# Hybrid decoder layer on one core: k's low part written once for two attentions, one projection copy moved to ScalarE, the down projection in token form

## The chip, the cores and the metric

The kernel runs on one core of a Trainium2 chip. The time is the device time of one execution in microseconds (us), as the median of several runs. The execution that the profiler recorded is one further run; its rows give times from the first instruction, and its span ends with the last one.

The names of the engines: PE is TensorE (PEld its weight loads), DVE is VectorE, ACT is ScalarE, POOL is GpSimd, SP is SyncE, which issues all the DMAs of this kernel.

## The reference

One decoder layer on 512 tokens of width 1024, in float32:

```python
a = rms_norm(h, attn_norm_g)
(nq, nkv, ngate, dq, dk, dv, fq, fk, fv, ff, mg) = split(a @ w_in)
# A: native sparse attention (compressed blocks, selected blocks, sliding window), 8 heads, gates from ngate
# B: differential attention, 4 heads x 2 maps;  C: forgetting attention, 8 heads, decay from ff
qb = rms_norm(dq per head of 64) * scale;  kb = rms_norm(dk per head of 64)
qc = rms_norm(fq per head of 64) * scale;  kc = rms_norm(fk per head of 64)
merged = gates[0] * (o_a @ w_br[0]) + gates[1] * (o_b @ w_br[1]) + gates[2] * (o_c @ w_br[2])
h = h + merged @ w_o
u, g = split(rms_norm(h, ffn_norm_g) @ w_up)         # 2816 features each
h = h + (gelu(causal_conv3(u)) * g) @ w_down
```

With 512 tokens the eight selected blocks are all the blocks there are, so the selected attention is causal attention over everything.

## The kernel before

**Precision.** A float32 product is made of three matmuls on fp32r operands. Each operand is cut into a high part (ACT rounds it, suffix `_h`, `wh`) and a low part (DVE subtracts the high part from the original, suffix `_l`, `wl`). The function `passes(dst, a_h, a_l, b_h, b_l, ...)` (L1278) issues high by high (L1280), high by low (L1281) and low by high (L1282). The first operand is the stationary one, the second moves through the array.

**Weights.** They come as 72 blocks of 128 x 2048 floats (1 MB each) through a ring of three raw buffers. ACT's `split` (L581, instruction at L588) writes `wh`, DVE's `split` (L849, instruction at L855) writes `wl` over the raw slot. SP loads a block when the block three places before has been used.

**The order of the work** is written out by hand for each engine, one instruction stream each, tied by semaphores. `place` gives each result its PSUM bank and its turn in it; `free` waits until a bank's result has been read, `full` until it has been written. The stages are: norm and transposes of x; for each of the three mixers (NSA, DIFF, FOX) its projections, its attention (a table of events in which gate-projection matmuls fill between the small attention steps) and its branch projection; the output projection; the FFN's up projection in 11 steps; the down projection in 11 blocks; the output.

**The start of NSA.** PE projects `cmp` (banks 6 and 7), `small` (32 columns for the gate and forget logits, bank 3), then the first half of `nq` for four token tiles into banks 0, 1, 2 and 3. The result of `small` is copied to `smT` by DVE (L917). In DVE's stream the copy stands behind `post(m, "cmp")` and the split of block `nq1`. PE then transposes `smT` (L1318), runs the first layer of the compression (`w1_sb` by `cpe`, L1335) and projects the second half of `nq`.

**q and k in DIFF and FOX.** After its norm a projection is transposed in four chunks of 128 columns (two heads of 64 each), each chunk by four PE transposes into bank 4 or 5 in turn (L1308). For k, ACT writes the high part of each head twice, into both halves of the partitions of `k_hh` (L656). DVE's `post_t` (L943 to L962) then writes the low part twice too:

```python
n = 2 * (chunk - 4) + e
hi = k_hh[home, n, :]
lows = [k_ll[home, n, :], k_ll[other, n, :]]
```

`q_hl` holds q's high part in a head's home half and its low part in the other half. So a score is one matmul with `k_hh` (high and low q by high k, L1422) and one with `k_ll` (high and low q by low k, L1423). Both `k_hh` and `k_ll` have eight heads' slots of 128 x 512. For NSA only slots 0 to 3 are used, and there both halves of `k_ll` are filled by one instruction (L864). DVE's stream after a k chunk pair is: 8 writes, the split of block `gate0`, 8 writes. On PE the first score of the attention waits until all chunks have been read (L1460 to L1464).

**The down projection** (`down`, L1603) has the stationary operand from the weights and the tokens moving, so the result for output columns `d` (8 groups of 128) has the features on the partitions and 512 tokens along the row, one bank each:

```python
cols = slice(d * P, (d + 1) * P)
ins = passes(ps[d][:, :], h[:, k, cols], l[:, k, cols], acts[k][0], acts[k][1], ...)
```

In the last block each finished bank is copied to `yT` (even `d` by ACT, L836, odd `d` by DVE, L1224), transposed back by four PE transposes (`finish`, L1597, two groups later in PE's stream), added to the residual `hid` into `outt` by DVE (L1217), and stored by SP in four stores of 256 columns each (L567).

Of the kernel before, what the change touches and what calls it, by code (L numbers as in the profile page):

```python
# [20 lines left out]
P = 128  # L21
S = 512
# [166 lines left out]
def build(nc, x, wblk, w1, w2, params, consts, out):  # L189
# [88 lines left out]
    for d in range(KD):  # L278
        plan(("YT", d), d)

    with ExitStack() as ctx:
# [73 lines left out]
        yT = at("yT", [P, KD, S], f32, 0)  # L355
        outt = at("outt", [P, TT, D], f32, 32 * KB)
# [77 lines left out]
        const_ready = sem("const_ready")  # L434
        cpe_ready = sem("cpe_ready")
# [101 lines left out]
        def _(sp):  # L537
# [27 lines left out]
            for n in range(4):  # L565
                sp.wait_ge(out_ready, 2 * n + 2)
                sp.dma_start(outv[:, :, n * 256:(n + 1) * 256], outt[:, :, n * 256:(n + 1) * 256]).then_inc(out_done, 16)  # L567
            sp.wait_ge(out_done, 64)
# [3 lines left out]
        def _(act):  # L572
# [125 lines left out]
            for m in (NSA, DIFF, FOX):  # L698
# [3 lines left out]
                if m == NSA:  # L702
                    split(BI[(m, "nq0")])
                    split(BI[(m, "nq1")])
# [128 lines left out]
            for d in range(0, KD, 2):  # L833
                full(act, ("Y", d))
                b = place[("Y", d)][0]
                nc.scalar.activation(yT[:, d, :], ps[b][:, :], ACT.Copy).then_inc(psum_free[b], 1)  # L836


        @block.vector
        def _(dve):  # L840
# [25 lines left out]
            def post(m, name):  # L866
# [47 lines left out]
                elif name == "small":  # L914
                    full(dve, ("P", m, name, 0))
                    b = place[("P", m, name, 0)][0]
                    nc.vector.tensor_copy(smT[:, :], ps[b][0:32, :]).then_inc(psum_free[b], 1)  # L917

            def post_t(m, name, part=0):
# [23 lines left out]
                for c in T_CHUNKS.get(name, [])[2 * part:2 * part + 2]:  # L943
# [7 lines left out]
                    for e in range(2):  # L951
# [4 lines left out]
                        else:  # L956
                            n = 2 * (chunk - 4) + e
                            hi = k_hh[home, n, :]
                            lows = [k_ll[home, n, :], k_ll[other, n, :]]
# [50 lines left out]
            for m in (NSA, DIFF, FOX):  # L1010
                units = units_of(m)
                if m == NSA:
# [3 lines left out]
                    post(m, "small")  # L1016
# [197 lines left out]
            def finish(d):  # L1214
                full(dve, ("YT", d))
                cols = slice(d * P, (d + 1) * P)
                nc.vector.tensor_tensor(outt[:, :, cols], bank(("YT", d))[:, :].rearrange("p (t c) -> p t c", t=TT), hid[:, :, cols],  # L1217
                                        ALU.add).then_inc(out_ready, 1)

            for d in range(KD):  # L1220
                if d % 2 == 1:
                    full(dve, ("Y", d))
                    b = place[("Y", d)][0]
                    nc.vector.tensor_copy(yT[:, d, :], ps[b][:, :]).then_inc(psum_free[b], 1)  # L1224
                if d >= 2:
                    finish(d - 2)
            finish(KD - 2)
            finish(KD - 1)


# [495 lines left out]
```

## Time and profile before

| What | us |
|---|---|
| median of 3 runs | 1049.41 (1049.34 to 1049.77) |
| the profiled execution, its own time | 1049.83 |
| its span, first to last instruction | 1047.9 |
| PE busy | 1014.6 (97%), 5133 matmuls |
| PEld busy | 850.4 (81%) |
| DVE busy | 576.9 (55%) |
| ACT busy | 413.0 (39%) |
| POOL busy | 80.8 (8%) |

PE's granted clock was 0.991 of full speed in the mean. A 512-column matmul is listed with about 0.39 us, but they overlap: a new one starts every 0.227 us at the full clock. So the start times tell the pace, and the listed durations don't. Idle time in a timeline row stands in brackets with what ended it.

### The profile page before, as it was taken

How to read it: one execution, taken by the hardware profiler on the slowest of the kernel's cores; microseconds unless marked ns; L12 is line 12 of the kernel's file. 1: busy time of each engine (PE TensorE's matmuls, PEld its weight loads, DVE VectorE, ACT ScalarE, POOL GpSimd, SP SyncE). 2: the span in 40 equal slices, each digit the busy share in tenths (PEclk: the TensorE clock that was granted, in tenths of full speed). 3: DMA queues.
4: the chain of work that ended last, by engine and by line, in shares of the span. 5: the costliest groups of instructions: out<-in, count | busy, mean ns of one | idle time of the engine just before them, and what ended most of it. 6: DMA issues, size and time to landing. Idle time of an engine off the chain costs nothing.

```text
span 1047.9 us, 13105 instructions
## 1 busy us (share of the span) xinstructions
PE 1014.6 (97%) x5133; PEld 850.4 (81%) x5133; DVE 576.9 (55%) x1056; ACT 413.0 (39%) x746; POOL 80.8 (8%) x66
## 2 busy tenths in 40 slices
PE   6899899999999999999899999999999999999998
PEld 5687789898887877888689888888888888888886
DVE  5645777773546678355655445465655656522123
ACT  4235445443446665424654433342322323221120
POOL 3200000000000000030000022011121111200000
PEclk9999899999999999999999999999999999999999
DMA  6512100102222211232211124222322323223222
GB/s 241 197 47 81 41 8 36 41 1 81 81 81 80 81 41 41 81 121 81 81 41 42 41 81 165 114 83 81 107 94 83 118 81 115 86 86 115 81 81 81
DMA packets 14653, 86.91 MB, mean 83 GB/s; under 512 B 1408, under 2 KB 3968, under 8 KB 5120
## 3 DMA queue, kind: packets, MB, share of 16 engines
q1 hardware_dynamic: 14592, 86.07, 23.1%
q8 instruction: 42, 0.69, 0.3%
q14 instruction: 19, 0.16, 0.1%
HBM read 83.96 MB, written 2.10 MB: 82 GB/s over the span
## 4 chain that ended last, share of the span: by engine, by line
PE 88%; DVE 7%; ACT 2%; issue 2%; DMA 1%; SPq 0%; DVEq 0%; ACTq 0%
PE ps L1280 20%; PE ps L1282 20%; PE ps L1281 20%; PE ps L1450 11%; PE ps L1436 5%; PE ps L1308 4%; PE ps L1422 2%; DVE k_ll L961 2%; PE ps L1423 2%; PE ps L1420 1%; DVE wl L855 1%; PE ps L1335 1%; PE ps L1413 1%; DVE nmx L1049 1%; DMA ident<-consts 1%
## 5 line engine op out<-in xcount | busy, mean ns | idle before, releaser
L855 DVE TENSOR_TENSOR wl<-raw,wh 128x512 fp32r<-128x512 f32 (+2 forms) x118 | 171.5, 1458 | 127.2 <-ACT wh L588 125.1
L588 ACT ACTIVATE wh<-raw 128x2048 fp32r<-128x2048 f32 (+1 forms) x58 | 109.4, 1886 | 155.9 <-PE ps L1282 138.3
L1280 PE MATMUL ps<-aT_h,wh 128*128 128x512 f32 (+1 forms) x376 | 146.7, 390 | 0.7 <-DVE aT_l L864 0.7
L1281 PE MATMUL ps<-aT_l,wh 128*128 128x512 f32 (+1 forms) x376 | 146.4, 389 | 0.0
L1282 PE MATMUL ps<-aT_h,wl 128*128 128x512 f32 (+1 forms) x376 | 146.4, 389 | 0.0
L737 ACT ACTIVATE prob<-ps,nmx 128x384 f32<-128x384 f32 (+3 forms) x128 | 66.7, 521 | 125.6 <-DVE nmx L1049 125.1
L1280 PE MATMUL ps<-wh,aT_h 128*128 128x512 f32 x256 | 102.4, 400 | 3.3 <-DVE smT L917 3.3
L1282 PE MATMUL ps<-wh,aT_l 128*128 128x512 f32 x256 | 101.1, 395 | 0.0
L1281 PE MATMUL ps<-wl,aT_h 128*128 128x512 f32 x256 | 100.9, 394 | 0.0
L1280 PEld LDWEIGHTS ps<-aT_h,wh 128*128 128x128 f32 (+1 forms) x376 | 70.0, 186 | 16.2 <-issue 0.9
L1282 PEld LDWEIGHTS ps<-aT_h,wl 128*128 128x128 f32 (+1 forms) x376 | 70.0, 186 | 15.3
L1281 PEld LDWEIGHTS ps<-aT_l,wh 128*128 128x128 f32 (+1 forms) x376 | 70.0, 186 | 15.2
L1436 PEld LDWEIGHTS ps<-V,probT 128*128 128x128 f32 x544 | 71.0, 193 | 11.8 <-DVE probT L1068 5.8
L1436 PE MATMUL ps<-V,probT 128*128 128x64 f32 (+1 forms) x544 | 75.6, 269 | 4.6 <-DVE probT L1068 3.1
L1450 PE MATMUL ps<-aT_h,wh 128*128 128x512 f32 x192 | 77.6, 404 | 0.8 <-DVE nrm L885 0.8
L1450 PE MATMUL ps<-aT_l,wh 128*128 128x512 f32 x192 | 77.9, 406 | 0.0
L1450 PE MATMUL ps<-aT_h,wl 128*128 128x512 f32 x192 | 77.4, 403 | 0.0
L1049 DVE TENSOR_REDUCE nmx<-ps 128x1 f32<-128x384 f32 (+3 forms) x128 | 61.3, 479 | 19.0 <-PE ps L1423 17.6
L1280 PE MATMUL ps<-actT_h,wh 128*128 128x512 f32 x176 | 68.9, 392 | 0.0
L1282 PE MATMUL ps<-actT_h,wl 128*128 128x512 f32 x176 | 68.5, 389 | 0.0
L1281 PE MATMUL ps<-actT_l,wh 128*128 128x512 f32 x176 | 68.5, 389 | 0.0
L1258 POOL TENSOR_TENSOR merged<-merged,bt 128x512 f32<-128x512 f32 x16 | 22.0, 1386 | 581.9 <-DVE bt L1139 581.9
(209 smaller groups left out, 1765.8 us busy)
## 6 DMA issues: line engine op xcount, KB each, us to landing
raw<-wblk SPq DMA_DIRECT2D x72, 1024.0 KB, 4.8
x<-x SPq DMA_DIRECT2D x4, 512.0 KB, 5.0
w_sb<-w SPq DMA_DIRECT2D x1, 2048.0 KB, 9.3
hid<-x SPq DMA_DIRECT2D x1, 2048.0 KB, 7.7
out<-outt SPq DMA_DIRECT2D x4, 512.0 KB, 3.1
stage<-consts SPq DMA_DIRECT2D x1, 1216.5 KB, 11.0
later<-consts SPq DMA_DIRECT2D x1, 448.0 KB, 12.0
par<-params SPq DMA_DIRECT2D x1, 204.5 KB, 7.8
```

What stands on the lines that cost most here:

```text
L588: nc.scalar.activation(wh[b % 2][:, 0:n], raw[b % RING][:, 0:n], ACT.Copy).then_inc(hi_ready, 4)
L737: nc.scalar.activation(prob[:, j % 4, 0:n], ps[b][:, 0:n], ACT.Exp, bias=nmx[:, j:j + 1], accum_out=lsum[:, j:j + 1]).then_inc(psum_free[b ...
L855: ins = nc.vector.tensor_tensor(wl[b % RING][:, cols], raw[b % RING][:, cols], wh[b % 2][:, cols].bitcast(f32), ALU.subtract)
L961: ins = nc.vector.scalar_tensor_tensor(dst, bank(key)[home, :], par[home, g:g + 1], hi.bitcast(f32), ALU.mult, ALU.subtract)
L1049: nc.vector.tensor_reduce(nmx[:, j:j + 1], bank(("S", m, j))[:, 0:n], AX.X, ALU.max, negate=True).then_inc(max_ready, 1)
L1258: nc.gpsimd.tensor_tensor(merged[:, c, :], merged[:, c, :], bt[:, c % 2, :], ALU.add).then_inc(merged_ready, 1)
L1280: nc.tensor.matmul(dst, a_h, b_h, start=start, stop=False)
L1281: nc.tensor.matmul(dst, a_h, b_l, start=False, stop=False)
L1282: return nc.tensor.matmul(dst, a_l, b_h, start=False, stop=stop)
L1308: ins = nc.tensor.transpose(bk[:, n * P:(n + 1) * P], src, ident[:, :])
L1436: ins = nc.tensor.matmul(bk[:, 0:vw], probT[:, pv_index(m, q) % 2, kb * P:(kb + 1) * P], V[:, s0 // P + kb, v0:v0 + vw], start=kb == 0, st ...
L1450: ins = nc.tensor.matmul(bk[:, :], (l if p == 2 else h)[:, k, cols], (aT_l if p == 1 else aT_h)[:, k], start=f % GATE_STEPS == 0, stop=f % ...
```

## The change

1. `k_ll` in DIFF and FOX: DVE writes only the home half of each head's slot. The other half is set to zero once, by two POOL memsets behind the last NSA score, and PE waits for that (`k_zero`) before the first DIFF score. The product of q's low part and k's low part is thereby no longer part of a DIFF or FOX score.
2. `smT` is copied by ACT, in front of its split of block `nq1`, and no longer by DVE.
3. The down projection has the activations as the stationary operand and the weights moving (512 output columns). Bank `d` then holds 128 tokens (tile `d // 2`) by 512 output columns (half `d % 2`), in the form of the output. `yT`, its copies and its 32 transposes are gone; DVE adds the residual from the bank directly, and SP stores each bank's 256 KB by itself, 8 stores for 4.

```diff
@@ scalar, NSA branch
                     split(BI[(m, "nq0")])
+                    full(act, ("P", m, "small", 0))
+                    b = place[("P", m, "small", 0)][0]
+                    nc.scalar.activation(smT[:, :], ps[b][0:32, :], ACT.Copy).then_inc(psum_free[b], 1)
                     split(BI[(m, "nq1")])
@@ scalar, end
-            for d in range(0, KD, 2):
-                full(act, ("Y", d))
-                b = place[("Y", d)][0]
-                nc.scalar.activation(yT[:, d, :], ps[b][:, :], ACT.Copy).then_inc(psum_free[b], 1)
@@ vector, post and NSA branch
-                elif name == "small":
-                    full(dve, ("P", m, name, 0))
-                    b = place[("P", m, name, 0)][0]
-                    nc.vector.tensor_copy(smT[:, :], ps[b][0:32, :]).then_inc(psum_free[b], 1)
...
-                    post(m, "small")
@@ vector, post_t
-                            lows = [k_ll[home, n, :], k_ll[other, n, :]]
+                            lows = [k_ll[home, n, :]]
@@ vector, end
             for d in range(KD):
-                if d % 2 == 1:
-                    full(dve, ("Y", d))
-                    b = place[("Y", d)][0]
-                    nc.vector.tensor_copy(yT[:, d, :], ps[b][:, :]).then_inc(psum_free[b], 1)
-                if d >= 2:
-                    finish(d - 2)
-            finish(KD - 2)
-            finish(KD - 1)
+                t, cols = d // 2, slice(d % 2 * S, d % 2 * S + S)
+                full(dve, ("Y", d))
+                nc.vector.tensor_tensor(outt[:, t, cols], bank(("Y", d))[:, :], hid[:, t, cols], ALU.add).then_inc(out_ready, 1)
@@ gpsimd
+            full(pool, ("S", NSA, len(units_of(NSA)) - 1))
+            nc.gpsimd.memset(k_ll[64:128, 0:8:2, :].bitcast(f32), 0.0)
+            nc.gpsimd.memset(k_ll[0:64, 1:8:2, :].bitcast(f32), 0.0).then_inc(k_zero, 1)
@@ tensor, first score
+                            if m == DIFF:
+                                pe.wait_ge(k_zero, 1)
@@ tensor, down
                 for d in range(KD):
                     if first:
                         begin(("Y", d))
-                    cols = slice(d * P, (d + 1) * P)
+                    rows, cols = slice(d // 2 * P, d // 2 * P + P), slice(d % 2 * S, d % 2 * S + S)
                     for k in range(2):
-                        ins = passes(ps[d][:, :], h[:, k, cols], l[:, k, cols], acts[k][0], acts[k][1], first and k == 0, last and k == 1)
+                        f = 2 * n + k
+                        ins = passes(ps[d][:, :], actT_h[:, f, rows], actT_l[:, f, rows], h[:, k, cols], l[:, k, cols],
+                                     first and k == 0, last and k == 1)
                     if last:
                         done(("Y", d), ins)
-                        if d >= 2:
-                            finish(d - 2)
@@ sync
-            for n in range(4):
-                sp.wait_ge(out_ready, 2 * n + 2)
-                sp.dma_start(outv[:, :, n * 256:(n + 1) * 256], outt[:, :, n * 256:(n + 1) * 256]).then_inc(out_done, 16)
-            sp.wait_ge(out_done, 64)
+            for d in range(KD):
+                t, cols = d // 2, slice(d % 2 * S, d % 2 * S + S)
+                sp.wait_ge(out_ready, d + 1)
+                sp.dma_start(outv[:, t, cols], outt[:, t, cols]).then_inc(out_done, 16)
+            sp.wait_ge(out_done, 16 * KD)
```

**Where the instructions stand.** ACT at the start of NSA, before. `wh`, `wl` and `raw` are the weight buffers, `ps` the PSUM banks, both with their numbers; a buffer's number behind the underscore is its place in memory only.

```order
L588 ACTIVATE wh1_58<-raw1_52 128x256 [waits raw_in1]
L588 ACTIVATE wh0_57<-raw2_53 128x2048 [waits raw_in2,psum_full7]
L588 ACTIVATE wh1_58<-raw0_51 128x2048 [waits raw_in0,psum_full3]
L633 ACTIVATE gsm_131<-smallt_130 128x96 [waits psum_free4,const_ready]
L635 ACTIVATE lf1_133<-logf_132 128x32 [waits small_v]
```

And of the change:

```order
L587 ACTIVATE wh1_58<-raw1_52 128x256 [waits raw_in1]
L587 ACTIVATE wh0_57<-raw2_53 128x2048 [waits raw_in2,psum_full7]
L705 ACTIVATE smT_77<-ps3 32x512 [waits psum_full3]
L587 ACTIVATE wh1_58<-raw0_51 128x2048 [waits raw_in0,psum_full3]
L632 ACTIVATE gsm_130<-smallt_129 128x96 [waits psum_free4,const_ready]
L634 ACTIVATE lf1_132<-logf_131 128x32 [waits small_v]
```

The copy of `smT` out of bank 3 is a new row between the splits of `nq0` and `nq1`; it waits for the same event as the split behind it (`psum_full3`). On DVE the same place, before:

```order
L904 MEMSET cpe_82 128x32 [waits psum_free7]
L911 TENSOR_TENSOR cpe_82<-cx_81,par_113 128x8x31 x4
L855 TENSOR_TENSOR wl0_54<-raw0_51,wh1_58 128x2048 [waits hi_ready]
L917 COPY smT_77<-ps3 32x512 [waits psum_full3]
L924 COPY smallt_130<-ps4 128x128 [waits psum_full4,const_ready]
L928 TENSOR_TENSOR logf_132<-smallt_130,par_113 128x32 [waits psum_free4]
```

And of the change:

```order
L901 MEMSET cpe_82 128x32 [waits psum_free7]
L908 TENSOR_TENSOR cpe_82<-cx_81,par_112 128x8x31 x4
L852 TENSOR_TENSOR wl0_54<-raw0_51,wh1_58 128x2048 [waits hi_ready]
L917 COPY smallt_129<-ps4 128x128 [waits psum_full4,const_ready]
L921 TENSOR_TENSOR logf_131<-smallt_129,par_112 128x32 [waits psum_free4]
```

The copy out of bank 3 is gone from behind DVE's split of `nq1`; nothing else moved.

DVE between the norm of DIFF's k and the first score of DIFF, before (`k_ll` rows of the same bank are one chunk, two heads):

```order
L855 TENSOR_TENSOR wl2_56<-raw2_53,wh1_58 128x2048 [waits hi_ready]
L961 SCALAR_TENSOR_TENSOR k_ll_70<-ps5,par_113,k_hh_69 64x512 [waits hi_taken]
L961 SCALAR_TENSOR_TENSOR k_ll_70<-ps5,par_113,k_hh_69 64x512 x3
L961 SCALAR_TENSOR_TENSOR k_ll_70<-ps4,par_113,k_hh_69 64x512 [waits hi_taken]
L961 SCALAR_TENSOR_TENSOR k_ll_70<-ps4,par_113,k_hh_69 64x512 x3
L855 TENSOR_TENSOR wl0_54<-raw0_51,wh0_57 128x2048 [waits hi_ready]
L961 SCALAR_TENSOR_TENSOR k_ll_70<-ps5,par_113,k_hh_69 64x512 [waits hi_taken]
L961 SCALAR_TENSOR_TENSOR k_ll_70<-ps5,par_113,k_hh_69 64x512 x3
L961 SCALAR_TENSOR_TENSOR k_ll_70<-ps4,par_113,k_hh_69 64x512 [waits hi_taken]
L961 SCALAR_TENSOR_TENSOR k_ll_70<-ps4,par_113,k_hh_69 64x512 x3
L1049 TENSOR_REDUCE nmx_122<-ps6 128x1 [waits psum_full6]
```

And of the change:

```order
L852 TENSOR_TENSOR wl2_56<-raw2_53,wh1_58 128x2048 [waits hi_ready]
L954 SCALAR_TENSOR_TENSOR k_ll_70<-ps5,par_112,k_hh_69 64x512 [waits hi_taken]
L954 SCALAR_TENSOR_TENSOR k_ll_70<-ps5,par_112,k_hh_69 64x512
L954 SCALAR_TENSOR_TENSOR k_ll_70<-ps4,par_112,k_hh_69 64x512 [waits hi_taken]
L954 SCALAR_TENSOR_TENSOR k_ll_70<-ps4,par_112,k_hh_69 64x512
L852 TENSOR_TENSOR wl0_54<-raw0_51,wh0_57 128x2048 [waits hi_ready]
L954 SCALAR_TENSOR_TENSOR k_ll_70<-ps5,par_112,k_hh_69 64x512 [waits hi_taken]
L954 SCALAR_TENSOR_TENSOR k_ll_70<-ps5,par_112,k_hh_69 64x512
L954 SCALAR_TENSOR_TENSOR k_ll_70<-ps4,par_112,k_hh_69 64x512 [waits hi_taken]
L954 SCALAR_TENSOR_TENSOR k_ll_70<-ps4,par_112,k_hh_69 64x512
L1041 TENSOR_REDUCE nmx_121<-ps6 128x1 [waits psum_full6]
```

Each chunk has two writes where it had four. The waits for ACT (`hi_taken`) and the place of the split of `gate0` are the same. FOX has the same rows.

PE at the end of the last down block, before:

```order
L1308 MATMUL ps4<-ident_111,yT_109 128x128 [waits psum_free4]
L1308 MATMUL ps4<-ident_111,yT_109 128x128 x3
L1280 MATMUL ps7<-actT_h_104,wh0_57 128x512
L1281 MATMUL ps7<-actT_l_105,wh0_57 128x512
L1282 MATMUL ps7<-actT_h_104,wl0_54 128x512
L1280 MATMUL ps7<-actT_h_104,wh0_57 128x512
L1281 MATMUL ps7<-actT_l_105,wh0_57 128x512
L1282 MATMUL ps7<-actT_h_104,wl0_54 128x512
L1308 MATMUL ps5<-ident_111,yT_109 128x128 [waits psum_free5]
L1308 MATMUL ps5<-ident_111,yT_109 128x128 x3
L1308 MATMUL ps6<-ident_111,yT_109 128x128 [waits psum_free6]
L1308 MATMUL ps6<-ident_111,yT_109 128x128 x3
```

And of the change:

```order
L1268 MATMUL ps6<-wh0_57,actT_l_105 128x512
L1266 MATMUL ps6<-wh0_57,actT_h_104 128x512
L1267 MATMUL ps6<-wl0_54,actT_h_104 128x512
L1268 MATMUL ps6<-wh0_57,actT_l_105 128x512
L1266 MATMUL ps7<-wh0_57,actT_h_104 128x512
L1267 MATMUL ps7<-wl0_54,actT_h_104 128x512
L1268 MATMUL ps7<-wh0_57,actT_l_105 128x512
L1266 MATMUL ps7<-wh0_57,actT_h_104 128x512
L1267 MATMUL ps7<-wl0_54,actT_h_104 128x512
L1268 MATMUL ps7<-wh0_57,actT_l_105 128x512
```

The transposes between and behind the matmul groups are gone; the matmuls are as many, with stationary and moving operand exchanged (the rows name the moving operand first).

## Rows read from the trace of the kernel before

**Rows 1.** The page, part 1: busy time, share of the span, instructions.
```profile
PE 1014.6 (97%) x5133; PEld 850.4 (81%) x5133; DVE 576.9 (55%) x1056; ACT 413.0 (39%) x746; POOL 80.8 (8%) x66
```
**Rows 2.** Waits of PE: us in total, times, longest.
```profile
PE ps L1308 <- DVE k_ll L961: 4.7, 2, 2.4
PE ps L1280 <- DVE smT L917: 3.3, 1, 3.3
```
**Rows 3.** Timeline of PE, start of NSA: start, us, instruction, [idle before].
```profile
40.36 0.39 PE L1282 MATMUL ps<-wh,aT_l 128*128 128x512 f32 x1
44.09 0.50 PE L1280 MATMUL ps<-wh,aT_h 128*128 128x512 f32 x1 [3.34 <-DVE smT L917]
...
48.60 0.43 PE L1318 MATMUL ps<-ident,smT 32*128 32x32 f32 x4
```
**Rows 4.** Timeline of ACT and DVE, same place.
```profile
32.65 1.92 ACT L588 ACTIVATE wh<-raw 128x2048 fp32r<-128x2048 f32 x1 [3.63 <-PE ps L1282]
...
39.59 1.53 DVE L911 TENSOR_TENSOR cpe<-cx,par 128x248 f32<-128x248 f32 x3
41.04 2.28 DVE L855 TENSOR_TENSOR wl<-raw,wh 128x2048 fp32r<-128x2048 f32 x1
43.35 0.68 DVE L917 COPY smT<-ps 32x512 f32<-32x512 f32 x1
```
**Rows 5.** One window: length, busy of PE, PEld, DVE, ACT, POOL, granted clock, DMA share, GB/s.
```profile
45.30:48.60 3.30, 3.30 (x9) 2.07 (x8) 0.00 (x0) 0.00 (x0) 0.00 (x0) 0.50 0.00 0
```
**Rows 6.** Timeline of ACT, PE and DVE, k of DIFF and its first score.
```profile
332.82 5.56 ACT L656 ACTIVATE k_hh<-ps,par 64x512 fp32r<-64x512 f32 x8
334.27 0.66 PE L1308 MATMUL ps<-ident,nrm 128*128 128x128 f32 x4 [2.36 <-DVE k_ll L961]
336.57 6.12 DVE L961 SCALAR_TENSOR_TENSOR k_ll<-ps,par,k_hh 64x512 fp32r<-64x512 f32 x8
342.94 0.30 PE L1420 MATMUL ps<-distD,slopeI 128*128 128x128 f32 x1
```
**Rows 7.** Timeline of ACT, DVE and PE, k of FOX and its first score.
```profile
509.16 5.57 ACT L656 ACTIVATE k_hh<-ps,par 64x512 fp32r<-64x512 f32 x8
512.90 6.12 DVE L961 SCALAR_TENSOR_TENSOR k_ll<-ps,par,k_hh 64x512 fp32r<-64x512 f32 x8
519.27 0.30 PE L1413 MATMUL ps<-fT,sel 128*128 128x128 f32 x1 [1.64 <-DVE k_ll L961]
```
**Rows 8.** Windows: DIFF's projections (weights moving), down projection (tokens moving).
```profile
314.00:324.00 10.00, 10.00 (x46) 8.29 (x45) 6.00 (x6) 3.63 (x7) 0.00 (x0) 1.00 0.31 105
1010.00:1020.00 10.00, 10.00 (x46) 8.29 (x45) 1.41 (x2) 1.92 (x1) 0.00 (x0) 1.00 0.08 31
```
**Rows 9.** Timeline of PE, last down block: first matmuls of two neighbouring groups.
```profile
1036.42 0.48 PE L1280 MATMUL ps<-actT_h,wh 128*128 128x512 f32 x1
...
1038.25 0.48 PE L1280 MATMUL ps<-actT_h,wh 128*128 128x512 f32 x1
```
**Rows 10.** Timeline of PE and DVE: last matmul, last copy, last adds.
```profile
1041.32 0.39 PE L1282 MATMUL ps<-actT_h,wl 128*128 128x512 f32 x1
1041.75 0.69 DVE L1224 COPY yT<-ps 128x512 f32<-128x512 f32 x1 [0.70 <-PE ps L1282]
1042.36 1.87 DVE L1217 TENSOR_TENSOR outt<-ps,hid 128x512 f32<-128x512 f32 x3
```
**Rows 11.** One window over the last two stores (columns of rows 5).
```profile
1044.00:1047.10 3.10, 0.00 (x0) 0.00 (x0) 0.23 (x1) 0.00 (x0) 0.00 (x0) 0.71 0.99 335
```
**Rows 12.** The page, part 6: the output stores, KB each, median us to landing.
```profile
out<-outt SPq DMA_DIRECT2D x4, 512.0 KB, 3.1
```
**Rows 13.** Timeline of POOL: a memset of 128 x 512.
```profile
25.61 0.53 POOL L1246 MEMSET fT<- 128x512 f32 x1
```
**Rows 14.** Two windows early in NSA's attention (columns of rows 5).
```profile
113.40:116.90 3.50, 3.50 (x11) 2.73 (x11) 1.70 (x6) 1.12 (x4) 0.00 (x0) 0.51 0.00 0
120.30:127.10 6.80, 6.31 (x22) 5.36 (x23) 5.04 (x19) 3.17 (x9) 0.00 (x0) 0.50 0.01 2
```

More of the change, by code:

```diff
@@ L277, in build @@
         plan(("Y", d), d)
-    for d in range(KD):
-        plan(("YT", d), d)
     with ExitStack() as ctx:
@@ L354, in build @@
         av = at("av", [P, 2, S], f32, RA + 96 * KB)
-        yT = at("yT", [P, KD, S], f32, 0)
-        outt = at("outt", [P, TT, D], f32, 32 * KB)
+        outt = at("outt", [P, TT, D], f32, 0)
         RK = RC + 19 * KB
@@ L434, in build @@
         const_ready = sem("const_ready")
+        k_zero = sem("k_zero")
         cpe_ready = sem("cpe_ready")
@@ L1212, in _ @@
                 split(B_DOWN + n)
-            def finish(d):
-                full(dve, ("YT", d))
-                cols = slice(d * P, (d + 1) * P)
-                nc.vector.tensor_tensor(outt[:, :, cols], bank(("YT", d))[:, :].rearrange("p (t c) -> p t c", t=TT), hid[:, :, cols],
-                                        ALU.add).then_inc(out_ready, 1)
-            for d in range(KD):
-                if d % 2 == 1:
-                    full(dve, ("Y", d))
-                    b = place[("Y", d)][0]
-                    nc.vector.tensor_copy(yT[:, d, :], ps[b][:, :]).then_inc(psum_free[b], 1)
-                if d >= 2:
-                    finish(d - 2)
-            finish(KD - 2)
-            finish(KD - 1)
+            for d in range(KD):
+                t, cols = d // 2, slice(d % 2 * S, d % 2 * S + S)
+                full(dve, ("Y", d))
+                nc.vector.tensor_tensor(outt[:, t, cols], bank(("Y", d))[:, :], hid[:, t, cols], ALU.add).then_inc(out_ready, 1)
         @block.gpsimd
@@ L1595, in _ @@
                         up_chunk(i, b, c)
-            def finish(d):
-                free(pe, ("Y", d))
-                transposes(("YT", d), [yT[:, d, t * P:(t + 1) * P] for t in range(TT)])
             def down(n):
@@ L1608, in down @@
                 h, l = [w[:, :].rearrange("p (k c) -> p k c", k=2) for w in (wh[blk % 2], wl[blk % RING])]
-                acts = [[t[:, 2 * n + k, :] for t in (actT_h, actT_l)] for k in range(2)]
                 for d in range(KD):
@@ L1612, in down @@
                         begin(("Y", d))
-                    cols = slice(d * P, (d + 1) * P)
+                    rows, cols = slice(d // 2 * P, d // 2 * P + P), slice(d % 2 * S, d % 2 * S + S)
                     for k in range(2):
-                        ins = passes(ps[d][:, :], h[:, k, cols], l[:, k, cols], acts[k][0], acts[k][1], first and k == 0, last and k == 1)
+                        f = 2 * n + k
+                        ins = passes(ps[d][:, :], actT_h[:, f, rows], actT_l[:, f, rows], h[:, k, cols], l[:, k, cols],
+                                     first and k == 0, last and k == 1)
                     if last:
                         done(("Y", d), ins)
-                        if d >= 2:
-                            finish(d - 2)
                 if not last:
@@ L1624, in _ @@
                 down(n)
-            finish(KD - 2)
-            finish(KD - 1)
 def pack_params(np, a):
```

## The prediction

> **What bounds the kernel now.** I read the page's busy times first. PE is busy 97% of the span [rows 1], so time can only be won where PE stands still, where its clock is low, where its work gets less, or behind its last instruction. The second view was the list of PE's waits. Of its waits on DVE or ACT the largest are two of 2.4 us for low parts of k (4.7 us) and one of 3.3 us for the copy of `smT` [rows 2]. Then I read the timeline around each place that the change touches: the start of NSA [rows 3, 4], k in DIFF and FOX [rows 6, 7], and the end [rows 9, 10]. A saving at one of these places should move everything behind it by as much, since from there on PE sets the pace; what may not move along is the clock (rivals below). The sum is made in the profiled execution, with its own time of 1049.83, 0.42 over the median of 1049.41. The savings are differences, so I take them off the median.
>
> **1. The copy of `smT`.** PE stops at 40.59 (the last matmul starts at 40.36, the next could 0.227 later) and goes on at 44.09 [rows 3]. What it wants is not `smT`: the fourth token tile of `nq` goes to bank 3, and there the result of `small` still waits for its copy. DVE reaches that copy only behind `cmp`'s work and the split of `nq1` (39.59, 41.04, then 43.35) [rows 4]. The result was there much earlier: ACT's split of `nq1`, which waits for the same event, starts at 32.65 [rows 4]. After the change ACT copies at 32.65 in at most the 0.68 that DVE needs, and bank 3 is free by 33.4, 7 us before PE asks. ACT's split of `nq1` ends 0.7 later, about 35.3, and DVE wants it at 41.04, so that costs nothing while DVE is late. The fourth tile starts at 40.59. Its 12 matmuls now take 48.60 - 44.09 = 4.5 us [rows 3], since after the stall the granted clock falls to 0.50 [rows 5], the level of 1.2 GHz; at 0.227 each they take 2.7. So the transposes of `smT` start near 40.59 + 2.72 + 0.1 = 43.4 instead of 48.60. **5.2 us.** Next in line is the compression's input, whose last row ends at 39.59 + 1.53 = 41.1 [rows 4], in time. Bounds: 3.3 (the idle time alone, if the clock falls anyway) and 5.3.
>
> **2. Low parts of k.** Each write takes 6.12 / 8 = 0.765 [rows 6], and 8 of 16 go in each of DIFF and FOX. The whole 6.1 per stage would come off only if DVE alone set the end. It doesn't: ACT's eight high parts behind its split run from 332.82 to 338.38 in DIFF [rows 6] and from 509.16 to 514.73 in FOX [rows 7], and nothing in the change makes them faster or earlier. The last chunk's low parts can start only then. In DIFF they end at 338.38 + 2 x 0.765 = 339.9; now the eight end at 336.57 + 6.12 = 342.7, and the first score starts at 342.94 [rows 6]. Gain 2.8. In FOX they end at 514.73 + 1.53 = 516.3 instead of 519.02, gain 2.8 [rows 7]. DVE's split of `gate0` comes before the pair and now starts when ACT's split ends (332.8 and 509.1), so it ends by 335.1 and 511.4, ahead of ACT's first chunk. PE must not be later than that: its second chunk pair stands behind a wait of 2.36 that ends when DVE has read the chunk before [rows 6]. With two writes fewer in each chunk that is at least 1.5 earlier, at 332.8. Behind it come transposes (0.4), 24 projection matmuls and 4 gate matmuls, 28 x 0.227 = 6.4: ready at 339.6, just before 339.9. Had PE the half clock there for 3 us, as behind the stall of [rows 5], it would be ready at 341.1 and DIFF would give 1.8. **5.6 us together**, bounds 3.6 (that, in both) and 12.2 (DVE alone).
>
> The zeros: a memset of 128 x 512 took 0.53 on POOL [rows 13]; two of four times the length are 4.2. They run behind NSA's last score, far ahead of DIFF's first at 342.94, on an engine that otherwise waits there. The wait for `k_zero` costs nothing. If they disturbed DVE for all of 4.2 us, that would fall where PE leads and DVE has gaps; nothing in the sum.
>
> **3. The down projection.** Matmuls stay 528, each with 512 columns and its own weight load. The form with weights moving is what the projections have now, and a 10 us stretch of it holds 46 matmuls, as a stretch of the down projection does [rows 8]; so the exchange costs nothing. In the last block the groups of two neighbouring banks start 1038.25 - 1036.42 = 1.83 apart [rows 9], of which six matmuls are 1.36. The four transposes between cost 0.47, and there are six such places: **2.8 us.** Behind the last matmul (start 1041.32) there come now a copy (1041.75), transposes, the last adds until 1042.36 + 1.87 = 1044.23 [rows 10], and 3.7 us until the span's end at 1047.9. After the change the add takes the copy's place: 0.43 + 0.69 = 1.12 behind the last matmul's start. What the last store takes is the open size. In the window 1044.0 to 1047.1 the last two stores, 1 MB, move at 335 GB/s [rows 11]; the last one starts behind the third. Alone and with half the bytes it needs 0.8 for its data, about 0.9 until they begin to move (the adds for the third store end at 1044.23 - 2 x 0.6 = 1043.0, and data move from 1044.0 on), and the same 0.8 from the last byte to the span's end: 2.5. So 3.6 instead of 6.6, **3.0 us**. Bounds: 1.8 (the last store as long as now) and 3.2.
>
> The median landing time of a 512 KB store is 3.1 us [rows 12], and its data alone need 1.6 of that at 335 GB/s. The Trainium skill's page "DMA: Bandwidth & Descriptors", section on the anatomy of one DMA, gives about 2.0 us fixed plus the bytes at 436 GB/s: 3.2 for 512 KB, close to the row, and 2.6 for 256 KB; with 2.6 until the landing and some 0.5 behind it the last store would take 3.1 instead of 2.5, and the time would be 1033.4.
>
> **Sum**: 5.2 + 5.6 + 2.8 + 3.0 = 16.6 us. 1049.41 - 16.6 = **1032.8 us**; the profiled execution's own time would be 1033.2.
>
> **The rivals.**
> *A. The clock early in NSA's attention goes another way.* The attention's start has two stretches at half the clock, 3.5 and 6.8 us [rows 14], behind short waits and small matmuls. With PE there 5.2 us earlier, the same waits fall into other stretches of the clock's record. If they no longer pull it down, up to 10.3 / 2 = 5.1 us come off: 1027.7. If one more stretch of 3.4 goes slow, 1.7 is lost: 1034.5. For it: behind waits of like length the clock did not always fall: FOX's matmuls behind the wait kept the full pace. Against: the same sparse work remains. 0.20 for a gain of over 2 us, 0.10 for a loss of 1 to 2.
> *B. Smaller terms.* The chunk pipeline gives less than ACT's row allows, or the fourth tile runs at half clock: down to 3.3 + 3.6 + 2.8 + 1.8 = 11.5, time 1037.9. 0.10.
> *C. The stores queue up.* If each store's whole time stood in a line, eight of about 2.5 behind the first add would end 7 x (2.5 - 1.36) = 8 us later than forecast: 1040.8. Against it: the last two stores' data moved without a gap within 3.1 us [rows 11], while one store alone takes 3.1 to land [rows 12], so their fixed parts overlap. The same page's section on bandwidth has the rule to batch transfers to 1 MB or more, and it speaks against cutting four stores into eight; by it this rival would come, and the trace's window is against it. 0.03.
> *D. Slower than before.* The moving operand of the down projection would now be `wh` and `wl`, which ACT and DVE are refilling meanwhile, and each step would take longer. From 16.6 / 528 = 31 ns more per matmul on, 0.258 instead of 0.227, the kernel is slower; at 40 ns it is 1053.9. Against it: the projections work like this now, with ACT and DVE busy beside them, at the same pace [rows 8]. 0.02.
> *E. The change doesn't do what it says*: bank 3 is not what PE waits for, so term 1 is missing and the time is 1038.0. The order of banks speaks against it. Counted in B.
>
> **How the numbers follow.** The forecast's own case, 1031 to 1035, has 0.55; A 0.30, B 0.10, C 0.03, D 0.02. The range from 1028.8 to 1037.0 leaves out the far end of A, the far end of B, C and D, together under 0.2. A measurement of this kernel tells about 0.2% (2 us) from no change; 1047.3 and below is faster. Faster 0.97, same 0.01, slower 0.02.
>
> **What the changed profile would show.** (1) PE's wait for `smT` is gone, no half clock near 45, transposes of `smT` near 43.4. (2) The first score of DIFF and of FOX starts 1.8 us behind ACT's last `k_hh` row, where it is now 4.6 behind. (3) 528 down matmuls 0.227 apart, the last block's groups 1.36 apart. (4) From the last matmul's start to the end of the span 3.6 us. The prediction is wrong if the early half-clock stretches [rows 14] change in length, if the down matmuls lose their pace, or if the last store still ends 3.7 us behind its add.

## The result and the profile after

The changed kernel takes **1032.28 us** (median of 4 runs, 1031.19 to 1033.83), beside 1049.38 (4 runs, 1049.29 to 1049.77) for the kernel before: ratio 0.9837, 95% interval 0.9820 to 0.9855. The forecast was 1032.8. The profiled execution took 1033.83, with a span of 1032.0; before it was 1049.83 and 1047.9.

The page of the changed kernel, part 1 and the first line of part 4 (the chain that ended last, by engine):

```profile
PE 1006.0 (97%) x5101; PEld 844.6 (82%) x5101; DVE 562.0 (54%) x1035; ACT 410.8 (40%) x743; POOL 84.5 (8%) x68
...
PE 90%; DVE 4%; ACT 4%; issue 1%; DMA 1%; SPq 0%; DVEq 0%; ACTq 0%
```

The matmuls are 32 fewer than in [rows 1], the transposes of `yT`. DVE's share of the chain was 7% before, ACT's 2%: more of what still holds PE up comes from ACT than before.

Its list of PE's waits, those that answer to [rows 2], and the longest one that the change didn't touch:

```profile
PE ps L1294 <- DVE k_ll L954: 1.7, 2, 0.9
PE ps L1294 <- DVE pc L1093: 1.7, 1, 1.7
...
PE ps L1406 <- DVE k_ll L954: 0.8, 1, 0.8
PE ps L1399 <- DVE k_ll L954: 0.7, 1, 0.7
```

The 3.3 for `smT` is gone, the two of 2.4 for `k_ll` have become two of 0.9. In front of the first scores 0.8 and 0.7 are left; [rows 7] had 1.64 for FOX.

The start of NSA, timelines of ACT, DVE and PE (compare [rows 3, 4]):

```profile
32.60 0.59 ACT L705 ACTIVATE smT<-ps 32x512 f32<-32x512 f32 x1 [3.58 <-PE ps L1268]
33.09 1.90 ACT L587 ACTIVATE wh<-raw 128x2048 fp32r<-128x2048 f32 x1
...
41.07 2.29 DVE L852 TENSOR_TENSOR wl<-raw,wh 128x2048 fp32r<-128x2048 f32 x1
...
43.40 0.43 PE L1304 MATMUL ps<-ident,smT 32*128 32x32 f32 x4
```

The fourth tile of `nq` as a window (columns of [rows 5], where its second part stood at 0.50):

```profile
40.60:43.40 2.80, 2.80 (x14) 2.06 (x12) 2.75 (x3) 0.00 (x0) 0.00 (x0) 1.00 0.00 0
```

k of DIFF and its first score, the same engines (compare [rows 6]):

```profile
327.64 5.57 ACT L655 ACTIVATE k_hh<-ps,par 64x512 fp32r<-64x512 f32 x8
333.24 2.06 ACT L625 ACTIVATE V<-ps 128x512 f32<-128x512 f32 x4
...
333.24 1.51 DVE L954 SCALAR_TENSOR_TENSOR k_ll<-ps,par,k_hh 64x512 fp32r<-64x512 f32 x2 [1.28 <-ACT k_hh L655]
...
333.92 0.39 PE L1436 MATMUL ps<-aT_h,wh 128*128 128x512 f32 x1
335.12 0.30 PE L1406 MATMUL ps<-distD,slopeI 128*128 128x128 f32 x1 [0.81 <-DVE k_ll L954]
```

Here one reads who sets the end. ACT's `k_hh` rows run without a gap until 333.21. DVE has waited 1.28 for the last of them, then writes the last two low parts until 334.75, and PE has waited 0.81 when the score starts at 335.12. So ACT's eight writes pace the stage, DVE adds its last two, and PE would be ready some 0.8 before.

One thing in this stage is not in [rows 6]: in the kernel before, PE's clock was down in it. Behind its wait of 2.36 come 3.4 us at half clock, in the changed kernel, where the wait is 0.87, none. Windows (columns of [rows 5]) of the kernel before and of the changed one:

```profile
335.30:338.70 3.40, 3.40 (x10) 2.63 (x9) 3.34 (x4) 3.31 (x6) 0.00 (x0) 0.50 0.00 0
```

```profile
327.30:334.10 6.80, 6.80 (x32) 5.55 (x32) 4.63 (x5) 6.65 (x11) 0.00 (x0) 1.00 0.00 0
```

There a matmul starts every 0.43 us for 0.227, so the 3.4 us cost PE about 1.7. So in DIFF it came to the first score only just when DVE had ended, with no idle time, while in FOX, at the full clock, it stood 1.64 [rows 7]. In the changed kernel FOX is as DIFF:

```profile
501.32 5.57 ACT L655 ACTIVATE k_hh<-ps,par 64x512 fp32r<-64x512 f32 x8
...
508.68 0.30 PE L1399 MATMUL ps<-fT,sel 128*128 128x128 f32 x1 [0.70 <-DVE k_ll L954]
```

POOL's memsets, far ahead of that:

```profile
234.68 1.80 POOL L1234 MEMSET k_ll<- 64x2048 f32 x1 [201.27 <-PE ps L1409]
236.51 1.80 POOL L1235 MEMSET k_ll<- 64x2048 f32 x1
```

The end, timelines of DVE and PE (compare [rows 9, 10]), and the stores on the page (compare [rows 12]):

```profile
1027.49 0.69 DVE L1209 TENSOR_TENSOR outt<-ps,hid 128x512 f32<-128x512 f32 x1 [0.67 <-PE ps L1268]
1028.85 0.69 DVE L1209 TENSOR_TENSOR outt<-ps,hid 128x512 f32<-128x512 f32 x1 [0.67 <-PE ps L1268]
...
1028.20 0.39 PE L1267 MATMUL ps<-wl,actT_h 128*128 128x512 f32 x1
1028.42 0.39 PE L1268 MATMUL ps<-wh,actT_l 128*128 128x512 f32 x1
```

```profile
out<-outt SPq DMA_DIRECT2D x8, 256.0 KB, 2.0
```

The adds, and with them the groups, are 1.36 apart (before 1.83, [rows 9]), and from the last matmul's start to the span's end it is 1032.0 - 1028.42 = 3.58 (before 6.58).

Differences of marks show where the 15.9 us between the two spans went. All marks are starts in PE's timeline of the profiled executions.

| From, to | before | after | gain | predicted |
|---|---|---|---|---|
| start, transposes of `smT` | 48.60 | 43.40 | 5.20 | 5.2 |
| to NSA's last score | 190.84 | 190.87 | -0.03 | 0 |
| to the first score of DIFF | 103.50 | 100.85 | 2.65 | 2.8 |
| to the first score of FOX | 176.33 | 173.56 | 2.77 | 2.8 |
| to the last matmul | 522.05 | 519.74 | 2.31 | 2.8 |
| to the end of the span | 6.58 | 3.58 | 3.00 | 3.0 |
| sum | 1047.9 | 1032.0 | 15.9 | 16.6 |

### The profile page after: what moved, and what is told of

Its sections match the earlier page's. It is cut to its first block, busy times and chain, and to the rows that moved or that the text cites. A ratio compares the mean times of both kernels' runs of the same rounds, so it can differ in the third digit from the quotient of the medians.

```text
span 1032.0 us, 13016 instructions
## 1 busy us (share of the span) xinstructions
PE 1006.0 (97%) x5101; PEld 844.6 (82%) x5101; DVE 562.0 (54%) x1035; ACT 410.8 (40%) x743; POOL 84.5 (8%) x68
## 4 chain that ended last, share of the span: by engine, by line
PE 90%; DVE 4%; ACT 4%; issue 1%; DMA 1%; SPq 0%; DVEq 0%; ACTq 0%
PE ps L1266 20%; PE ps L1268 20%; PE ps L1267 20%; PE ps L1436 11%; PE ps L1422 5%; PE ps L1294 4%; ACT k_hh L655 2%; PE ps L1408 2%; PE ps L1409 2%; PE ps L1406 1%; DVE wl L852 1%; PE ps L1321 1%; DMA ident<-consts 1%; PE ps L1399 1%; DVE nmx L1041 1%
## 5 line engine op out<-in xcount | busy, mean ns | idle before, releaser
L1266 PE MATMUL ps<-wh,actT_h 128*128 128x512 f32 x176 | 68.5, 389 | 0.0
L1267 PE MATMUL ps<-wl,actT_h 128*128 128x512 f32 x176 | 68.5, 389 | 0.0
L1268 PE MATMUL ps<-wh,actT_l 128*128 128x512 f32 x176 | 68.5, 389 | 0.0
L1249 POOL TENSOR_TENSOR gl<-gl,rstdT 128x512 f32<-128x512 f32 x22 | 44.5, 2022 | 234.6 <-ACT gl L826 234.6
```

The costliest lines, as they stand in the source:

```text
L1249: nc.gpsimd.tensor_tensor(gl[:, c, :], gl[:, c, :], rstdT[:, :], ALU.mult).then_inc(glr_ready, 1)
L1266: nc.tensor.matmul(dst, a_h, b_h, start=start, stop=False)
L1267: nc.tensor.matmul(dst, a_h, b_l, start=False, stop=False)
L1268: return nc.tensor.matmul(dst, a_l, b_h, start=False, stop=stop)
```

## The experiments

Two theories stand for each term: the one of the prediction, and one in which another engine or resource sets the size. Each changed piece was run alone first, from the kernel before. The four below ran on one chip, where the kernel before took 1049.05 (13 runs, 1047.31 to 1050.41).

### The low parts alone

```diff
-                            lows = [k_ll[home, n, :], k_ll[other, n, :]]
+                            lows = [k_ll[home, n, :]]
@@ gpsimd
+            full(pool, ("S", NSA, len(units_of(NSA)) - 1))
+            nc.gpsimd.memset(k_ll[64:128, 0:8:2, :].bitcast(f32), 0.0)
+            nc.gpsimd.memset(k_ll[0:64, 1:8:2, :].bitcast(f32), 0.0).then_inc(k_zero, 1)
@@ tensor, first score
+                            if m == DIFF:
+                                pe.wait_ge(k_zero, 1)
```

> Part 1 of the change alone (home half of k_ll written, zeros by POOL; the product of low q and low k is left out in DIFF and FOX). My theory: ACT's high parts pace the chunks, so DIFF and FOX give 2.7 each, 1049.4 - 5.5 = 1043.9, and the first score starts 1.9 us behind ACT's last k_hh row in both. Rival, DVE alone sets the end: 12 us, 1037.4. Rival, the two waits move to another place and the time stays: 1049.

1044.2 us (1042.12 to 1045.15), ratio 0.9948 (0.9932 to 0.9965), 4.9 less. The stage to DIFF's first score takes 340.98 - 240.13 = 100.85, the one to FOX's 514.58 - 340.98 = 173.60: 2.65 and 2.73 less than before. That DVE alone set the end, which would give 12, falls, and so does that the waits only move.

### The copy of `smT` alone

```diff
@@ scalar, between the splits of nq0 and nq1
+                    nc.scalar.activation(smT[:, :], ps[b][0:32, :], ACT.Copy).then_inc(psum_free[b], 1)
@@ vector
-                    post(m, "small")
```

> Part 2 alone (smT copied by ACT). My theory: the stall and the half clock behind it go, 5.2 us, 1044.2, and the transposes of smT start at 43.4. If the terms of the change add up, the stretches of half clock early in NSA behave as after the whole change: in some runs about 2 us less, then 1042. Rival, only the idle time goes: 3.3 us, 1046.1.

1043.52 us (1042.75 to 1045.31), ratio 0.9951 (0.9936 to 0.9965), 5.5 less. The transposes of `smT` start at 44.17; this execution's rows stand 0.7 later from the start on (ACT's copy is at 33.37), so the gain there is 48.60 + 0.72 - 44.17 = 5.15, as in the whole change. The clock moves two other stages of this execution, and they cancel: NSA's takes 1.8 less than before (3.4 us at half clock in it for 10.2), and from FOX's first score to the last matmul it takes 1.7 more (3.4 us at half clock from 513.7 on, for none).

### The down projection alone

Part 3 of the change as it stands there, with the adds and the eight stores. Its core:

```diff
-                        ins = passes(ps[d][:, :], h[:, k, cols], l[:, k, cols], acts[k][0], acts[k][1], first and k == 0, last and k == 1)
+                        ins = passes(ps[d][:, :], actT_h[:, f, rows], actT_l[:, f, rows], h[:, k, cols], l[:, k, cols],
+                                     first and k == 0, last and k == 1)
```

> Part 3 alone (down projection in token form, eight stores). My theory: 2.8 us from the transposes in the last block and 3.1 behind the last matmul, 5.9 together, 1043.5; nothing ahead of the down projection moves, so the early half-clock stretches stay in every run and the spread stays under 1 us. Rival, the form costs or gives something per matmul: the 528 matmuls of the down projection are not 0.227 apart.

1044.67 us (1043.94 to 1044.79), ratio 0.9958 (0.9943 to 0.9973), 4.4 less where 5.9 were expected. The marks give 5.3: from FOX's first score to the last matmul 1039.30 - 519.55 = 519.75 (2.3 less), from there to the end 3.6 (3.0 less). Of the 0.6 between 5.9 and 5.3, 0.5 is a miscount (below). The 0.9 between 5.3 and 4.4 isn't settled: the marks are taken against the first profile of the kernel before, whose own time of 1049.83 is 0.8 over the median of the same kernel on this chip, and executions differ by as much. The pace of the matmuls, the matter of rival D, is the same in both forms: 0.227 from start to start. A window in the down projection of the changed kernel (columns of [rows 5], compare [rows 8]):

```profile
1000.00:1010.00 10.00, 10.00 (x46) 8.29 (x45) 1.41 (x2) 1.92 (x1) 0.00 (x0) 1.00 0.03 11
```

### Another bank for `small`

In the kernel before, the result of `small` goes to bank 4, and DVE copies it as late as ever. If PE waits for `smT` itself, nothing is won by that; if it waits for bank 3, most of term 1 is.

```diff
-            plan(("P", m, "small", 0), 3)
+            plan(("P", m, "small", 0), 4)
```

> The kernel before with one number changed: the result of small goes to bank 4 instead of 3, DVE still copies it late. My theory: PE waited for the bank and not for smT, so the fourth token tile runs without a wait; behind it PE waits only from 43.4 to 44.1 for smT itself, and about 4.5 us come off, 1044.9. Rival, PE waits for smT: PE stands until 44.1 as before and nothing or little (under 1 us) is won.

The times decide nothing: 1047.61 in the median of 10 runs, but from 1043.63 to 1051.61; ratio 0.9991 (0.9970 to 1.0012). The trace does, timelines of DVE and PE:

```profile
42.06 2.29 DVE L855 TENSOR_TENSOR wl<-raw,wh 128x2048 fp32r<-128x2048 f32 x1
44.38 0.68 DVE L917 COPY smT<-ps 32x512 f32<-32x512 f32 x1
...
44.07 0.39 PE L1282 MATMUL ps<-wh,aT_l 128*128 128x512 f32 x1
45.21 0.40 PE L1318 MATMUL ps<-ident,smT 32*128 32x32 f32 x4 [0.75 <-DVE smT L917]
```

The fourth tile of `nq` runs to its end (44.07) while DVE is still at the split of `nq1`. PE waits for `smT` only where it reads it, 0.75 at 45.21. So the 3.3 of [rows 2] were a wait for the bank, though the row names only the copy that frees it; rival E falls. Counted from DVE's rows, which stand 1.0 later here than in [rows 4], the transposes start 4.4 earlier than before. The copy on ACT gives the other 0.8 as well.

The times fall into two groups, five from 1043.63 to 1045.03 us with a mean clock of 0.997 or 0.992, and five from 1050.18 to 1051.61 with 0.986 to 0.990. So the lower clock goes with the longer time, but it doesn't account for all of it: 0.002 of clock, from 0.992 (1045.01) to 0.990 (1051.61), can cost 2 us by my estimate (0.002 x 1048; 3 with the rounding of the two clocks), and 6.6 us lie between. Only an execution of the first group was profiled, so what sets the second apart stays open.

### The changed kernel again, and who paces k

The next four ran on a second chip, where the kernel before took 1048.94 (7 runs, 1047.1 to 1049.23). The changed kernel itself:

> The changed kernel once more, for the size of its spread on this chip and as the mark for the three others. My theory: the terms of the change are fixed and the rest is the clock: executions with a granted clock near 1.0 take about 1031.2, those with stretches at half clock longer, by half the length of the stretches that PE fills, 1033 to 1034 with 10 us of them. Rival, the spread has nothing to do with the clock: the times don't follow it.

1031.67 us (1030.21 to 1033.0), ratio 0.9839 (0.9823 to 0.9855).

If ACT's eight `k_hh` writes pace the stage, taking two of them (the second copy of every other head) to DVE must move the score. If DVE paces it, the added work makes it later.

```diff
@@ scalar, k_hh of head e of a chunk
-                            for r in range(2):
+                            for r in (range(2) if e == 0 else (1,)):
@@ vector, post_t
+                            if e == 1:
+                                nc.vector.tensor_copy(k_hh[other, n, :], hi.bitcast(f32))
```

> The changed kernel, and ACT gives one of its four k_hh writes per chunk to DVE (a copy of the half just written). My theory: ACT's row of eight paces the first score now, so with six it ends 1.4 earlier twice per stage; PE's own work becomes the bound near 333.4, and DIFF and FOX give 1.6 each, 3.2 together, against the changed kernel on the same chip. Rival, DVE paces: its four writes per chunk pair become six, and the first score comes no earlier or up to 1 us later.

1028.58 us (1026.36 to 1029.3), ratio 0.9807 (0.9791 to 0.9822), 3.1 less than the changed kernel. Timelines of ACT, DVE and PE ahead of DIFF's first score:

```profile
325.81 4.18 ACT L655 ACTIVATE k_hh<-ps,par 64x512 fp32r<-64x512 f32 x6 [0.22 <-PE ps L1296]
...
330.77 0.42 DVE L954 CAST k_hh<-k_hh 64x512 fp32r<-64x512 f32 x1
331.21 0.76 DVE L956 SCALAR_TENSOR_TENSOR k_ll<-ps,par,k_hh 64x512 fp32r<-64x512 f32 x1
...
332.34 0.39 PE L1438 MATMUL ps<-aT_h,wh 128*128 128x512 f32 x1
332.57 0.22 PE L1408 MATMUL ps<-distD,slopeI 128*128 128x128 f32 x1
```

ACT has six writes for eight, the low parts end at 331.97, and the score follows the last matmul 0.23 later with no idle time. The stages to the first scores of DIFF and FOX take 98.94 and 171.67, that is 1.9 less each than in the changed kernel, 3.8 together. ACT had paced them; now PE does, and more off ACT or DVE here would give nothing.

### The early half clock of NSA

Rival A was that the half-clock stretches of [rows 14] change. In the profiled execution of the changed kernel they are there, about 4.9 us earlier than before, and as PE itself is 5.2 us earlier, they lie over almost the same work; in that of the same kernel on the second chip they are not there. The same windows of both (columns of [rows 5]), first the changed kernel's first profile:

```profile
108.70:112.10 3.40, 3.40 (x13) 2.79 (x12) 1.47 (x6) 1.33 (x4) 0.00 (x0) 0.52 0.27 43
115.50:122.40 6.90, 6.85 (x26) 5.86 (x27) 5.02 (x20) 3.54 (x12) 0.00 (x0) 0.51 0.00 0
```

and its second:

```profile
108.70:112.10 3.40, 3.40 (x27) 3.10 (x25) 1.73 (x7) 1.52 (x6) 0.00 (x0) 1.00 0.42 128
115.50:122.40 6.90, 5.58 (x35) 4.09 (x33) 6.55 (x25) 3.33 (x12) 0.00 (x0) 1.00 0.00 0
```

At the full clock (1.00, the 2.4 GHz level) PE does 27 matmuls in the first window, at 0.52 (1.2 GHz) 13. The stage from `smT`'s transposes to NSA's last score takes 190.87 with the slow stretches and 187.92 without. The 10.3 us at half clock thus cost 3.0 and not the 5.1 that I had bounded with them: at the full clock PE stands idle for 1.3 of the second window, so part of that time was not PE's to win.

Does the clock fall because of the wait ahead of it? The last longer wait before these stretches is the 1.7 for `pc` in the list above. Against it speaks that the second profile, without slow stretches, has it too (PE's timeline), and so has the profile of the run with another bank (1.70 at 108.31), where NSA has no half clock either:

```profile
106.29 0.44 PE L1294 MATMUL ps<-ident,pc 128*128 128x128 f32 x2 [1.69 <-DVE pc L1093]
```

So I filled it: 8 of the 24 gate matmuls that stand ahead of NSA's first score were moved to between the second and the third score, where that wait is.

```diff
-HEAD_FILL = {NSA: 24, DIFF: 4, FOX: 4}
+HEAD_FILL = {NSA: 16, DIFF: 4, FOX: 4}
@@ the table of events, for j in range(slots)
-    n = FILL - tail - head
+    extra = 8 if m == NSA else 0
+    n = FILL - tail - head - extra
+    def upto(j):
+        return head + n * j // slots + (extra if j >= 2 else 0)
-        put_fill(j, head + n * j // slots, head + n * (j + 1) // slots)
+        put_fill(j, upto(j), upto(j + 1))
```

> The changed kernel with the gate-projection matmuls early in NSA's attention set differently: 8 fewer ahead of the first transposes of the sw chunks, 8 more between the second and the third score, where PE waits 1.7 us for the compressed probabilities. Theory of the clock (the half-clock stretches follow waits): the wait goes and with it most of the half clock, 1.7 plus up to 2.4 us less than the changed kernel, and a smaller spread. Rival, the sparse small matmuls make the clock fall and not the wait: 1.7 us less at most, the stretches stay.

1031.13 us (1028.62 to 1031.58), ratio 0.9827 (0.9809 to 0.9844), 0.5 less in the median. The wait is gone, and between executions of like clock that is worth about 2: the profiled one takes 188.56 in NSA's stage, 2.3 less than the 190.87 of the changed kernel with as much half clock. But the half clock stayed, one stretch of 3.4 us from 140.8 on and the longer one here:

```profile
113.80:120.60 6.80, 6.80 (x28) 5.80 (x27) 5.41 (x21) 3.36 (x11) 0.00 (x0) 0.52 0.00 0
```

Two of its four executions had a mean clock of 0.995, one 0.997, one 1.0, which is no other mixture than the changed kernel's (0.995, 0.997, 0.998, 1.0 on the same chip). My theory that the clock follows this wait falls.

### Four stores in token form

Are eight small stores better than four large ones of the same form?

```diff
-            for d in range(KD):
-                t, cols = d // 2, slice(d % 2 * S, d % 2 * S + S)
-                sp.wait_ge(out_ready, d + 1)
-                sp.dma_start(outv[:, t, cols], outt[:, t, cols]).then_inc(out_done, 16)
+            for t in range(TT):
+                sp.wait_ge(out_ready, 2 * t + 2)
+                sp.dma_start(outv[:, t, :], outt[:, t, :]).then_inc(out_done, 16)
... (the last wait goes with the number of stores)
```

> The changed kernel with four stores of 512 KB instead of eight of 256 KB. My theory: only the last store counts, and its data take 0.7 us longer, so the span after the last matmul's start grows from 3.6 to 4.3. Rival (small stores cost more, larger ones pay): it stays or gets shorter.

1033.18 us (1032.36 to 1033.58), ratio 0.9853 (0.9838 to 0.9868), 1.5 over the changed kernel in the median, of which the traces show 0.6 at the end: from the last matmul, in PE's timeline,

```profile
1026.87 0.39 PE L1267 MATMUL ps<-wh,actT_l 128*128 128x512 f32 x1
```

to the span's end at 1031.0 it is 4.13, against 3.51 and 3.58 in two profiles of the changed kernel. The stores on its page:

```profile
out<-outt SPq DMA_DIRECT2D x4, 512.0 KB, 2.6
```

The rest of the 1.5 is within what executions differ by. The last store's data move for 1.43 us here and for 0.82 in the changed kernel (below), which is the 0.6. What counts is how much data is left when the last add ends, so the last store should be small.

### Both additions together

The copies of `k_hh` shared between ACT and DVE and the filled wait of NSA, both edits as above, on a third chip (the kernel before: 1049.36, 7 runs, 1047.79 to 1049.96), with the changed kernel beside them.

> The changed kernel with both edits, the shared k_hh writes and the moved gate matmuls. My theory: they act at different places, 3.8 us from the first and 1.7 to 2.3 from the second by their traces, so about 5.7 below the changed kernel's ratio of 0.984, which is 0.978 or 1026.2 against 1049. The half-clock stretches in NSA stay in some executions, with a spread of 3 us. Rival (with the wait gone PE is earlier and runs into a later wait on DVE, so the second edit gives nothing here): 0.980, 1028.

> The changed kernel beside it on the same chip: ratio 0.984 to the kernel before, and again 1030 to 1031 at a granted clock near 1.0, 1033 to 1034 where about 10 us go at half clock.

The version with both takes **1026.01 us** (1024.65 to 1026.31), ratio 0.9777 (0.9763 to 0.9792); the changed kernel took 1032.94 there (1032.07 to 1033.3), ratio 0.9843 (0.9827 to 0.9860). So both together give 6.9 more; alone on the second chip they gave 3.1 and 0.5 in the medians. By the marks, k gives 1.9 + 1.9 as alone. NSA's stage takes 187.63 for 190.71, 3.1 less, but the two traces have 3.4 and 6.8 us at half clock there. The run with four stores, without the filled wait, has 3.4 us too and takes 189.26. So 1.6 of the 3.1 are the filled wait by these traces (2.3 by those above), and the rest goes with the clock. It is the fastest version of this study.

## Why the prediction was right, by its steps

**What bounds the kernel.** Right. PE sets the pace behind each of these places, and no saving was given back: NSA's stage, which lies between two of them, took the same time within 0.03 us, with as much half clock in it (10.2 us) in both traces.

**Term 1, 5.2.** 5.20, with both of its parts. The idle 3.3 is gone, and so is the half clock behind it: the transposes start at 43.40, as worked out. That the wait was for bank 3 was argued from the order of banks, and is shown by the run with another bank.

**Term 2, 5.6.** 5.42 in the changed kernel, 5.38 alone. ACT's row was the right one to go by: the score starts 335.12 - 333.21 = 1.9 behind it, 1.8 was forecast. The missing 0.15 in DIFF is nearly all in the time from DVE's last low part to the score: 0.37 now, 0.25 before [rows 6]; with the low parts alone it is 0.36. That PE now restarts from a wait doesn't explain it, for FOX's score starts from a wait in both kernels, 0.25 behind DVE each time. What DIFF's first score has and FOX's has not is the new wait for `k_zero`. It was put at nothing; no run leaves it out, so that it costs this 0.1 is not shown. The memsets were not late: they took 3.6 for the 4.2 estimated and ended 97 us ahead of that score.

PE was ready in time, at the full clock, so the bound of 3.6 didn't come. Here the prediction was lucky: it had half clock in this stage as something that might come, and saw no row of it, but in DIFF it was there already, 3.4 us behind the wait of 2.36. It went when that wait shrank, and nothing in the prediction said why it should. Had it stayed, PE would have been ready 1.7 later than its 334.15 (my estimate), 0.7 behind the actual score.

**Term 3, the six places at 0.47.** This is the step that was off. "There are six such places" counts the transposes that stand behind the last matmul group too; those had been counted once already in the 6.6 from the last matmul to the end. Ahead of the last matmul stand five: 5 x 0.47 = 2.3, measured 2.31. The exchange of the operands cost nothing, as the window of the projections had told.

**The end, 3.0.** 3.00, from 6.58 to 3.58. The last store's whole time behind its add is 1032.0 - 1029.54 = 2.5, the value built from the trace, and its three parts of 0.9, 0.8 and 0.8 came too. Windows of the changed kernel from the end of the last add, over the store's data, and to the end of the span (columns of [rows 5]):

```profile
1029.54:1030.40 0.86, 0.00 (x0) 0.00 (x0) 0.00 (x0) 0.00 (x0) 0.00 (x0) 1.00 0.25 91
1030.40:1031.22 0.82, 0.00 (x0) 0.00 (x0) 0.00 (x0) 0.00 (x0) 0.00 (x0) 1.00 0.84 317
1031.22:1031.96 0.74, 0.00 (x0) 0.00 (x0) 0.00 (x0) 0.00 (x0) 0.00 (x0) 1.00 0.00 0
```

(The 91 GB/s of the first are the end of the store before.) The Trainium skill's page "DMA: Bandwidth & Descriptors" (the anatomy of one DMA) gives 2.6 until the landing of 256 KB, and with that the end would have come 0.6 later; the median landing was 2.0, so here the trace was the better guide. For the 512 KB of the four stores the page gives 3.2, and 2.6 were measured. The page states this sum for DMAs that GpSimd issues, and SP issues these, which the prediction didn't say. The same page's rule to batch to 1 MB or more is about the share of the peak bandwidth, on loads that GpSimd issues; it says nothing of a queue, so rival C did not follow from it. For the last transfer of this kernel the larger stores cost 0.6 us. Rival C did not come: the stores were issued 1.36 apart and landed 2.0 after their issue (median), so one was under way while the next began.

**Rival A** came in part, and makes up for the rest. By the marks 15.9 us are gained and the median fell by 17.1, since the executions shown differ: two had a mean clock of 0.995 (1033.23, 1033.83), two of 1.0 (1031.19, 1031.33), and the median lies between them. So the forecast of 1032.8 was hit by two errors of opposite sign: 0.7 too much in the terms, and some 1 us that executions differ by, which goes with a clock that was held to be fixed. That the executions at 1.0 are those without the two stretches of NSA is seen in one profile of each kind; what decides which kind an execution becomes stays open. The wait of 1.7 ahead of them doesn't decide it.

**Rivals B, D and E** did not come: terms 1 and 2 and the end stayed well above their lower bounds, the down matmuls kept their pace, and bank 3 was what PE waited for.

## What to carry to other kernels

A saving on an engine that feeds the bound is worth only the distance to the next engine in the row: here DVE's writes were halved (6.1 us per stage), and ACT's unchanged row let 2.8 through; read off the second engine's last instruction before counting. When a wait names a copy, look whose bank or buffer the waiting instruction writes: another bank had freed the fourth tile without touching the copy. When one pass counts gaps up to the last instruction and another the time behind it, name the instruction where the one ends and the other begins, or the border is counted twice.

## What the runs showed of the hardware

The granted clock of TensorE is not a constant of a kernel, not even on one chip. The kernel before had 0.990 to 0.995 and 1047.31 to 1050.41 us in 13 runs; the version with `small` in bank 4 had 0.986 to 0.997, and 1043.63 to 1051.61 us, in 10. A median of few runs then tells 1 or 2 us less surely than two traces compared mark by mark, as long as each stage's clock is read beside it.

The same wait is not always followed by half clock. All four traces in which PE waits 2.36 for the low parts in both stages (the kernel before, the copy alone, the down projection alone, the other bank) have 3.4 us at half clock behind it in DIFF, and none of them has any behind it in FOX. None of the eight traces in which that wait is 0.87 or less has half clock there. So shortening the wait took the half clock away each time, but the wait's length alone doesn't tell whether it comes.
